# Second projection of a two-layer diffusion transformer: rows and sums split into two parts before they are stored

## The chip, the cores and the metric

The kernel runs on one core of one Trainium2 chip. The metric is the device time of one execution in microseconds (us), lower is better. Three runs of the kernel before gave 3569.83, 3571.33 and 3574.09 us, median 3571.33. The profiled execution of the same kernel took 3568.55 us.

## The reference, cut to what matters

The whole model is two layers over 256 context and 2048 latent tokens, width 1024. The change touches one product of the second layer, `h @ w_in`, where h (2304 x 1024) is the modulated layer norm of the first layer's output and the matrix gives q, k, v, o, z (1024 columns each) and 16 gates:

```python
h_lat = layer_norm(x) * (1.0 + sc_l[:, None, :]) + sh_l[:, None, :]
q, k, v, o, z, g = jnp.split(h @ w_in, ODD_SPLITS, axis=-1)
y = jax.nn.sigmoid(o) * hsum.reshape(b, t, MLSTM_W).astype(o.dtype) * jax.nn.silu(z)
```

## The kernel before, in words

Every f32 product is made of three matmuls over operands split in two parts: the high part is the value rounded to the matmul's f32 type (`ACT.Copy` into an F32R tile, on ScalarE), the low part is the value minus the high part (VectorE). `split_mm` (lines 319 to 321) adds high x high, high x low and low x high.

The second projection has two stages, each a block with a barrier at its end.

Stage one, `queries_and_sums` (tiles named `pa_`), takes 128-token tiles in pairs: eight latent pairs (0 to 7), then the context pair (8). For each tile: TensorE transposes the normalised rows (`turned`, line 1529), ScalarE and VectorE modulate half each into `ht` (lines 1401 and 1494), ScalarE makes the high part (1409), VectorE the low part (1500). Per latent pair TensorE runs four query steps of 48 matmuls and, between them, two gate products (`gates`, line 1541) into one PSUM tile, which ScalarE copies out before the next (`gate_out`, 1423). The query steps' sums are copied to `stage` (1415) and stored. The order of one pair on TensorE is: step, transposes, step, transposes, gates, step, gates, step. GpSimd forms four sums per pair from the quarters of the two tiles (1468), for a product scheme with seven products in place of eight (Strassen's, in Winograd's form), and afterwards the inverse deviations that the next pair's normalisation on VectorE waits for. It also forms three of the weight sums (`w_add`, line 1240) after pairs 3, 5 and 7, and ScalarE makes the high part of the first two of them (`w_high`, 1248) at the end of pairs 3 and 5. SyncE's queue stores to the DRAM tensor `s_hsum` three quarters of the raw rows (1335, 1337) and the four sums (1341, two buffers), whole and unsplit. Context tiles aren't split in this stage.

Stage two, `seven_products` (tiles named `pb_`), runs 34 units (four column groups over the pairs), each of seven products of 12 matmuls: 238 groups. For each group ScalarE's queue loads one 128 x 512 quarter (1659), ScalarE makes its high part (1665), VectorE its low part (1765), TensorE multiplies. Each quarter is so split anew in each column group. VectorE, ScalarE and GpSimd combine the seven results (1689 to 1797, 1743, 1747) and gate them. In the last unit of a column group ScalarE and VectorE also split the next group's weights (1248, 1253). The first unit's weights 3 to 6 are split at the stage's start; GpSimd makes the low parts of 4 and 5 (1253).

Semaphores alone set the order between engines; each engine runs its instructions in the order written. `sum_stored`, `row_stored`, `lo_done` and `mm_done` are the ones that the change touches.

## Time and profile before

| | |
|---|---|
| median of three runs | 3571.33 us |
| profiled execution, its time / its span | 3568.55 / 3566.8 us |
| TensorE matmul busy | 3367.9 us, 94% |
| VectorE, ScalarE, GpSimd busy | 66%, 38%, 50% |
| stage one (`pa_`), in the trace | about 2063 to 2289 us |
| stage two (`pb_`), in the trace | 2289 to 2981 us |

Times in the rows are microseconds from the start of the span. In a timeline a row is one or more merged instructions: start, length, engine, line, operation, tiles written and read, and in brackets the idle time of the engine just before it and what ended it. PEld is TensorE's weight load, SPq and ACTq are the DMA-issuing queues of SyncE and ScalarE. A matmul's listed length is longer than the distance between two starts, since they overlap.

### The profile page before, as it was taken

How to read it: one execution, taken by the hardware profiler on the slowest of the kernel's cores; microseconds unless marked ns; L12 is line 12 of the kernel's file. 1: busy time of each engine (PE TensorE's matmuls, PEld its weight loads, DVE VectorE, ACT ScalarE, POOL GpSimd, SP SyncE). 2: the span in 40 equal slices, each digit the busy share in tenths (PEclk: the TensorE clock that was granted, in tenths of full speed). 3: DMA queues.
4: the chain of work that ended last, by engine and by line, in shares of the span. 5: the costliest groups of instructions: out<-in, count | busy, mean ns of one | idle time of the engine just before them, and what ended most of it. 6: DMA issues, size and time to landing. Idle time of an engine off the chain costs nothing. (4 is left out here: it accounts for less than half of the span.)

```text
span 3566.8 us, 49291 instructions
## 1 busy us (share of the span) xinstructions
PE 3367.9 (94%) x16144; PEld 2481.1 (70%) x16144; DVE 2367.9 (66%) x3521; ACT 1359.8 (38%) x2274; POOL 1772.2 (50%) x1205
## 2 busy tenths in 40 slices
PE   7999998799999999999979979899999998999898
PEld 5788885555555555555568779777878786887686
DVE  4666543778877777777757754356575644779665
ACT  3433335444444444444420033334443422665300
POOL 1033312577777777777724333422575512445354
PEclk8999998799999999999989989999999999999999
DMA  5335545511111111111255555555545446768663
GB/s 206 114 110 140 139 145 171 168 33 33 37 32 35 36 34 35 36 34 35 62 172 177 175 170 181 193 191 163 172 138 170 152 148 200 218 209 274 233 229 130
DMA packets 358838, 475.43 MB, mean 133 GB/s; under 512 B 57932, under 2 KB 212444, under 8 KB 358512
## 3 DMA queue, kind: packets, MB, share of 16 engines
q1 hardware_dynamic: 300736, 359.32, 32.3%
q10 hardware_dynamic: 51600, 94.16, 8.9%
q0 software_dynamic: 6304, 19.42, 1.4%
q8 instruction: 111, 1.82, 0.2%
q14 instruction: 87, 0.71, 0.1%
HBM read 337.32 MB, written 135.36 MB: 133 GB/s over the span
## 5 line engine op out<-in xcount | busy, mean ns | idle before, releaser
L2419 DVE TENSOR_REDUCE al_mx<-al_sx 128x1 f32<-128x512 f32 (+1 forms) x960 | 559.1, 631 | 202.0 <-PE al_sx L2522 192.2
L2339 ACT ACTIVATE al_e<-al_st 128x1024 f32<-128x1024 f32 x432 | 443.3, 1027 | 535.6 <-PE al_st L2537 535.2
L2388 POOL TENSOR_TENSOR al_acc_p<-al_acc_p,al_e 128x1024 f32<-128x1024 f32 x188 | 455.7, 2424 | 19.8 <-POOL al_acc_p L2388 0.9
L319 PE MATMUL pb_acc<-p_whi,pb_r_hi 128*128 128x512 f32 x952 | 376.9, 396 | 31.7 <-DVE pb_r_lo L1765 22.4
L2546 PE MATMUL al_acc<-al_e,vres 128*64 128x512 f32 x1728 | 402.5, 601 | 0.0
L321 PE MATMUL pb_acc<-p_whi,pb_r_lo 128*128 128x512 f32 x952 | 373.7, 393 | 0.0
L320 PE MATMUL pb_acc<-p_wlo,pb_r_hi 128*128 128x512 f32 x952 | 373.6, 392 | 0.0
L2536 PE MATMUL al_st<-al_qa,kres 128*128 128x512 f32 x864 | 346.5, 401 | 3.8 <-issue 3.2
L2537 PE MATMUL al_st<-al_qb,kres 128*128 128x512 f32 x864 | 340.9, 395 | 0.0
L1765 DVE TENSOR_TENSOR pb_r_lo<-pb_stg,pb_r_hi 128x512 fp32r<-128x512 f32 x238 | 218.4, 919 | 168.5 <-ACT pb_r_hi L1665 164.5
L2522 PE MATMUL al_sx<-kres,al_qx 128*128 128x512 f32 (+1 forms) x960 | 310.7, 396 | 9.8 <-DVE al_mx L2419 7.6
L2522 PEld LDWEIGHTS al_sx<-kres,al_qx 128*128 128x128 f32 x960 | 170.7, 189 | 171.4 <-issue 114.9
L2382 POOL TENSOR_TENSOR al_acc_p<-al_e 128x1024 f32<-128x1024 f32 x48 | 160.8, 3351 | 223.9 <-ACT al_e L2339 223.9
L2546 PEld LDWEIGHTS al_acc<-al_e,vres 128*64 128x64 f32 x1728 | 111.2, 136 | 211.5 <-issue 195.6
L1665 ACT ACTIVATE pb_r_hi<-pb_stg 128x512 fp32r<-128x512 f32 x238 | 149.4, 628 | 268.3 <-PE pb_acc L321 252.0
L319 PEld LDWEIGHTS pb_acc<-p_whi,pb_r_hi 128*128 128x128 f32 x952 | 180.1, 189 | 77.2 <-DVE pb_r_lo L1765 29.1
L319 PE MATMUL mo_acc<-ow_whi,mo_y_hi 128*128 128x512 f32 x544 | 215.5, 396 | 4.9 <-DVE mo_y_lo L3088 4.9
L321 PE MATMUL mo_acc<-ow_whi,mo_y_lo 128*128 128x512 f32 x544 | 214.0, 393 | 0.0
L320 PE MATMUL mo_acc<-ow_wlo,mo_y_hi 128*128 128x512 f32 x544 | 213.9, 393 | 0.0
L2536 PEld LDWEIGHTS al_st<-al_qa,kres 128*128 128x128 f32 x864 | 162.8, 188 | 70.8 <-issue 29.1
L973 DVE TENSOR_TENSOR pj_h_lo<-pj_hall,pj_h_hi 128x1024 fp32r<-128x1024 f32 x90 | 116.4, 1310 | 138.2 <-ACT pj_h_hi L841 138.2
L321 PEld LDWEIGHTS pb_acc<-p_whi,pb_r_lo 128*128 128x128 f32 x952 | 180.1, 189 | 39.6
(344 smaller groups left out, 7411.6 us busy)
## 6 DMA issues: line engine op xcount, KB each, us to landing
pb_stg<-s_hsum ACTq DMA_DIRECT2D x238, 256.0 KB, 2.8
s_proj<-pb_out SPq DMA_DIRECT2D x72, 256.0 KB, 3.3
p_wst<-in_w1s ACTq DMA_DIRECT2D x18, 1024.0 KB, 5.5
ml_k<-s_proj SPq DMA_DIRECT2D x36, 512.0 KB, 4.4
ml_v<-s_proj SPq DMA_DIRECT2D x36, 512.0 KB, 8.9
hm_w<-in_ada_w SPq DMA_DIRECT2D x16, 1024.0 KB, 7.8
ml_qt<-s_qt SPq DMA_DIRECT2D x32, 512.0 KB, 6.4
mo_in<-s_h SPq DMA_DIRECT2D x32, 512.0 KB, 4.6
```

The source lines that it names most:

```text
L319: nc.tensor.matmul(out, s_hi, m_hi, start=start, stop=False)
L320: nc.tensor.matmul(out, s_hi, m_lo, start=False, stop=False)
L321: return nc.tensor.matmul(out, s_lo, m_hi, start=False, stop=stop)
L1765: V.tensor_tensor(r_lo[:, g % RING], stg[:, g % NSTG], r_hi[:, g % RING].bitcast(F32), ALU.subtract).then_inc(lo_done, 1)
L2339: nc.scalar.activation(e[:, pair(p, j), :, :], st[(NP * p + j) % 2][:, :, 0:W], ACT.Exp).then_inc(e_done, 1)
L2382: nc.gpsimd.tensor_tensor(acc_p[:], e[:, pair(p, 2)], e[:, pair(p, 5)], ALU.add).then_inc(add_p, 1)
L2388: nc.gpsimd.tensor_tensor(acc_p[:], acc_p[:], e[:, pair(p, j)], ALU.add).then_inc(add_p, 1)
L2419: V.tensor_reduce(mx[:, x:x + 1], slots[x % NSX][:, 0:spans[x % NS][1]], AX.X, ALU.max).then_inc(sx_max, 1)
L2522: mm(slots[x % NSX][:, 0:width], qx[:, p, i * P:(i + 1) * P], kres[:, g, lo:lo + width], start=True, stop=True).then_inc(sx_mm, 1)
L2536: mm(dst[:, t, 0:W], kres[:, g, keys], qa[:, p, :], start=True, stop=False)
L2537: y = mm(dst[:, t, 0:W], kres[:, NKV + g, keys], qb[:, p, :], start=False, stop=True)
L2546: y = mm(acc[t * HD:(t + 1) * HD, 0:W], vres[:, 2 * j + t, g, :], e[:, pair(p, j), t, :], start=(j == 0), stop=(j == NP - 1))
```

## The change

It moves the splits of rows and sums from stage two into stage one. `s_hsum` doubles in size: each quarter now has a high and a low plane (`(NT // 2, 7, P, 2, CH)`).

Stage one now splits the context tiles too. The stores of rows read `h_hi` and `h_lo` (four DMAs a pair instead of two, twice the bytes), so `ht` is freed without waiting for a store, and `h_hi`/`h_lo` wait for it instead. GpSimd's four sums have a buffer each (`sums`, four places), ScalarE writes the high part to `sum_hi` (two places), VectorE subtracts in place. These splits of a pair's sums stand one pair later in each engine's order (`early_splits`), but those of pair 7 in pair 7 (`late_splits`) and those of pair 8 at the end. A sum's split in a `sum_hi` place waits until the place's last content is stored. The loads of the next rows (`load_x`) are issued ahead of the sums' stores. `stage` has two places instead of three.

Stage two loads both parts of a quarter in one DMA of 512 KB into a ring of six (instead of four raw and four split), with no split; TensorE waits for the DMA. Weights 4 and 5 of the first unit get their low parts on VectorE, and the order of the weights' splits there is 3, 4, 5, 6.

ScalarE, stage one, from the end of pair 3 into pair 4. `pa_stage` is the copy of a query step, `p_whi` the high part of the weight sum, `pa_ht` a modulated tile, `pa_h_hi` its high part, `pa_gst` the copy of a gate product.

```order
L1415 ACTIVATE pa_stage<-pa_acc 128x512
L1248 ACTIVATE p_whi<-p_wst 128x2048
L1415 ACTIVATE pa_stage<-pa_acc 128x512
L1401 ACTIVATE pa_ht<-pa_tp,keep_mod 128x128 x4
L1409 ACTIVATE pa_h_hi<-pa_ht 128x1024
L1415 ACTIVATE pa_stage<-pa_acc 128x512
L1401 ACTIVATE pa_ht<-pa_tp,keep_mod 128x128 x4
L1409 ACTIVATE pa_h_hi<-pa_ht 128x1024
L1423 ACTIVATE pa_gst<-pa_gacc,pa_gbias 128x128
```

The same place after the change:

```order
L1420 ACTIVATE pa_stage<-pa_acc 128x512
L1248 ACTIVATE p_whi<-p_wst 128x2048
L1420 ACTIVATE pa_stage<-pa_acc 128x512
L1436 ACTIVATE pa_sum_hi<-pa_sums 128x512 x2
L1407 ACTIVATE pa_ht<-pa_tp,keep_mod 128x128 x4
L1414 ACTIVATE pa_h_hi<-pa_ht 128x1024
L1420 ACTIVATE pa_stage<-pa_acc 128x512
L1436 ACTIVATE pa_sum_hi<-pa_sums 128x512 x2
L1407 ACTIVATE pa_ht<-pa_tp,keep_mod 128x128 x4
L1414 ACTIVATE pa_h_hi<-pa_ht 128x1024
L1428 ACTIVATE pa_gst<-pa_gacc,pa_gbias 128x128
```

Two pairs of splits of the pair before now stand ahead of the two modulations, and so ahead of the gate copy that TensorE's second gate product waits for.

SyncE's queue, stage one, its last DMAs, from the store of the third query step of pair 7 on. Before:

```order
L1352 DMA s_qt<-pa_stage 128x2x256
L1346 DMA s_graw<-pa_gst 128x128
L1341 DMA s_hsum<-pa_sums 128x512 x2
L1352 DMA s_qt<-pa_stage 128x2x256
L1346 DMA s_graw<-pa_gst 128x128 x2
```

After:

```order
L1363 DMA s_qt<-pa_stage 128x2x256
L1357 DMA s_graw<-pa_gst 128x128
L1352 DMA s_hsum<-pa_sum_hi 128x512
L1352 DMA s_hsum<-pa_sums 128x512
L1352 DMA s_hsum<-pa_sum_hi 128x512
L1352 DMA s_hsum<-pa_sums 128x512
L1363 DMA s_qt<-pa_stage 128x2x256
L1352 DMA s_hsum<-pa_sum_hi 128x512
L1352 DMA s_hsum<-pa_sums 128x512
L1352 DMA s_hsum<-pa_sum_hi 128x512
L1352 DMA s_hsum<-pa_sums 128x512
L1357 DMA s_graw<-pa_gst 128x128
```

Behind the last query store (`s_qt`) stood two gate stores. Now there stand four stores of the context pair's sums 0 and 1, a gate store, and behind these rows four more of its sums 2 and 3 and the last gate store.

VectorE at the start of stage two. Before:

```order
L1765 TENSOR_TENSOR pb_r_lo<-pb_stg,pb_r_hi 128x512 x2
L1253 TENSOR_TENSOR p_wlo<-p_wst,p_whi 128x2048
L1765 TENSOR_TENSOR pb_r_lo<-pb_stg,pb_r_hi 128x512 x3
L1780 TENSOR_TENSOR pb_u<-pb_acc,pb_s 128x512
```

After:

```order
L1253 TENSOR_TENSOR p_wlo<-p_wst,p_whi 128x2048 x2
L1233 TENSOR_TENSOR p_wst<-p_wst 128x2048
L1253 TENSOR_TENSOR p_wlo<-p_wst,p_whi 128x2048 x2
L1790 TENSOR_TENSOR pb_u<-pb_acc,pb_s 128x512
```

All four low parts of weights and the last weight sum (1233) now stand ahead of the first result.

```diff
-        self.ops = q + [(0, i) for i in (0, 2, 1, 3, 4, 6, 5)] + [(p, i) for p in range(1, 4) for i in range(7)]
+        self.ops = q + [(0, i) for i in (0, 2, 1, 3, 4, 5, 6)] + [(p, i) for p in range(1, 4) for i in range(7)]
...
-    tag, NX, RING, NH, NACC, NST = "pa_", 2, 4, 4, 3, 3
+    tag, NX, RING, NH, NACC, NST = "pa_", 2, 4, 4, 3, 2
...
-    sums = m.sb(tag + "sums", [P, 2, 4, P])
+    sums, sum_hi = m.sb(tag + "sums", [P, 4, 4, P], F32R), m.sb(tag + "sum_hi", [P, 2, 4, P], F32R)
...
+    sum_done, sum_stored, row_stored = m.sem(tag + "sum"), m.sem(tag + "sum_stored", 4), m.sem(tag + "row_stored")
+    sum_hi_done, sum_lo_done = m.sem(tag + "sum_hi"), m.sem(tag + "sum_lo")
+    early_splits = lambda pair, b: [(pair - 1, 2 * b), (pair - 1, 2 * b + 1)] if 0 < pair < LAT else [(LAT, 2 * b), (LAT, 2 * b + 1)] if pair == LAT else []
+    late_splits = lambda pair, b: [(pair, 2 * b), (pair, 2 * b + 1)] if pair == LAT - 1 else []
...
-            eng.wait_ge(row_stored, 32 * pair + 32)
-            if pair < LAT:
-                eng.wait_ge(hi_done, i - NH + 1)
-                eng.wait_ge(lo_done, i - NH + 1)
+            eng.wait_ge(hi_done, i - NH + 1)
+            eng.wait_ge(lo_done, i - NH + 1)
+
+    def split_free(eng, i):
+        if i >= RING:
+            eng.wait_ge(mm_done, 4 * ((i - RING) // 2 + 1))
+            eng.wait_ge(row_stored, 64 * ((i - RING) // 2 + 1))
...
             def rows(pair):
-                modulated(sp, 2 * pair)
                 view = s["hsum"][pair]
-                sp.dma_start(view[0:2].rearrange("o p f -> p o f"), ht[:, 2 * pair % NH].rearrange("p (o k) n -> p o (k n)", o=2)).then_inc(row_stored, 16)
-                modulated(sp, 2 * pair + 1)
-                sp.dma_start(view[2], ht[:, (2 * pair + 1) % NH, 4:KD].rearrange("p k n -> p (k n)")).then_inc(row_stored, 16)
-
-            def sum_out(pair, n):
-                sp.wait_ge(sum_done, 4 * pair + n + 1)
-                sp.dma_start(s["hsum"][pair, 3 + n], sums[:, n % 2].rearrange("p k n -> p (k n)")).then_inc(sum_stored[n % 2], 16)
+                for i in (2 * pair, 2 * pair + 1):
+                    for part, (done, t) in enumerate(((hi_done, h_hi), (lo_done, h_lo))):
+                        sp.wait_ge(done, i + 1)
+                        if i % 2 == 0:
+                            sp.dma_start(view[0:2, :, part].rearrange("o p f -> p o f"), t[:, i % RING].rearrange("p (o k) n -> p o (k n)", o=2).bitcast(F32)).then_inc(row_stored, 16)
+                        else:
+                            sp.dma_start(view[2, :, part], t[:, i % RING, 4:KD].rearrange("p k n -> p (k n)").bitcast(F32)).then_inc(row_stored, 16)
+
+            def sum_out(pair, q):
+                sp.wait_ge(sum_lo_done, 4 * pair + q + 1)
+                view = s["hsum"][pair, 3 + q]
+                for part, t in enumerate((sum_hi[:, q % 2], sums[:, q])):
+                    sp.dma_start(view[:, part], t.rearrange("p k n -> p (k n)").bitcast(F32)).then_inc(sum_stored[q], 16)
...
             for pair in range(LAT):
                 last = pair == LAT - 1
                 rows(pair)
-                sum_out(pair, 0)
-                sum_out(pair, 1)
-                query_out(4 * pair)
-                if not last:
-                    load_x(2 * pair + 4)
-                sum_out(pair, 2)
-                query_out(4 * pair + 1)
-                if not last:
-                    load_x(2 * pair + 5)
-                sum_out(pair, 3)
-                gate_out(2 * pair)
-                if last:
-                    rows(PAIRS - 1)
-                    sum_out(PAIRS - 1, 0)
-                    sum_out(PAIRS - 1, 1)
-                query_out(4 * pair + 2)
-                gate_out(2 * pair + 1)
-                if last:
-                    sum_out(PAIRS - 1, 2)
-                    sum_out(PAIRS - 1, 3)
-                query_out(4 * pair + 3)
+                for b in range(2):
+                    query_out(4 * pair + b)
+                    if not last:
+                        load_x(2 * pair + 4 + b)
+                    for of in early_splits(pair, b):
+                        sum_out(*of)
+                for b in range(2):
+                    gate_out(2 * pair + b)
+                    for of in late_splits(pair, b):
+                        sum_out(*of)
+                    if last and b == 0:
+                        rows(PAIRS - 1)
+                    query_out(4 * pair + 2 + b)
                 if pair in (1, 2, 4, 6):
                     w.w_load(sp, (0, {1: 0, 2: 2, 4: 1, 6: 3}[pair]))
-            gate_out(2 * LAT)
-            gate_out(2 * LAT + 1)
+            for b in range(2):
+                for of in early_splits(LAT, b):
+                    sum_out(*of)
+                gate_out(2 * LAT + b)
...
+            def sum_high(pair, q):
+                act.wait_ge(sum_done, 4 * pair + q + 1)
+                if q >= 2:
+                    act.wait_ge(sum_stored[q - 2], 32 * pair + 32)
+                elif pair:
+                    act.wait_ge(sum_stored[q + 2], 32 * pair)
+                nc.scalar.activation(sum_hi[:, q % 2], sums[:, q].bitcast(F32), ACT.Copy).then_inc(sum_hi_done, 1)
...
                     i = 2 * pair + 2 + b
                     if q:
                         query_out(4 * pair + b)
+                    for of in early_splits(pair, b):
+                        sum_high(*of)
                     if i < NT:
                         modulate(i)
-                        if i < 2 * LAT:
-                            high(i)
+                        high(i)
                 for b in range(2):
                     gate_out(2 * pair + b)
+                    for of in late_splits(pair, b):
+                        sum_high(*of)
                     if q:
                         query_out(4 * pair + 2 + b)
...
-                terms = ((a21, a22, ALU.add), (sums[:, 0], a11, ALU.subtract), (a11, a21, ALU.subtract), (a12, sums[:, 1], ALU.subtract))
-                for n, (p, q, op) in enumerate(terms):
-                    if pair or n >= 2:
-                        pool.wait_ge(sum_stored[n % 2], 16 * (2 * pair + n // 2))
-                    if n:
-                        pool.wait_ge(sum_done, 4 * pair + n)
-                    G.tensor_tensor(sums[:, n % 2], p, q, op).then_inc(sum_done, 1)
+                place = [sums[:, n].bitcast(F32) for n in range(4)]
+                terms = ((a21, a22, ALU.add), (place[0], a11, ALU.subtract), (a11, a21, ALU.subtract), (a12, place[1], ALU.subtract))
+                for q, (x, y, op) in enumerate(terms):
+                    if pair:
+                        pool.wait_ge(sum_stored[q], 32 * pair)
+                    if q:
+                        pool.wait_ge(sum_done, 4 * pair + q)
+                    G.tensor_tensor(place[q], x, y, op).then_inc(sum_done, 1)
...
+            def sum_low(pair, q):
+                dve.wait_ge(sum_hi_done, 4 * pair + q + 1)
+                if q < 2:
+                    dve.wait_ge(sum_done, 4 * pair + (2, 4)[q])
+                place = sums[:, q]
+                V.tensor_tensor(place, place.bitcast(F32), sum_hi[:, q % 2].bitcast(F32), ALU.subtract).then_inc(sum_lo_done, 1)
...
+    tag, RING = "pb_", 6
...
             def load(g):
                 u, i = divmod(g, 7)
-                if g >= NSTG:
-                    act.wait_ge(lo_done, g - NSTG + 1)
-                act.dma_start(stg[:, g % NSTG].rearrange("p k n -> p (k n)"), s["hsum"][UNITS[u][1], w.ROWS[i]]).then_inc(ld[g % NSTG], 16)
-
-            def high(g):
-                act.wait_ge(ld[g % NSTG], 16 * (g // NSTG) + 16)
                 if g >= RING:
                     act.wait_ge(mm_done, g - RING + 1)
-                nc.scalar.activation(r_hi[:, g % RING], stg[:, g % NSTG], ACT.Copy).then_inc(hi_done, 1)
+                act.dma_start(rows[:, g % RING].rearrange("p w k n -> p w (k n)").bitcast(F32), s["hsum"][UNITS[u][1], w.ROWS[i]]).then_inc(ld[g % RING], 16)
...
                 nc.scalar.activation(sg[:, at % 2], out[:, kind], ACT.Sigmoid).then_inc(sg_done[kind], 1)

-            for g in range(NSTG):
+            for g in range(3):
                 load(g)
-            for g in range(2):
-                high(g)
             w.w_high(act, (0, 3))
-            for g in range(2, RING):
-                high(g)
-            for g in range(NSTG, NSTG + RING - 1):
+            for g in range(3, RING):
                 load(g)
+            w.w_high(act, (0, 4))
...
-                if j + NSTG + RING - 1 < N:
-                    load(j + NSTG + RING - 1)
-                if j in (0, 2, 3):
-                    w.w_high(act, (0, {0: 4, 2: 6, 3: 5}[j]))
+                if j + RING < N:
+                    load(j + RING)
...
-            for g in range(2):
-                low(g)
             w.w_low(V, (0, 3))
-            for g in range(2, RING):
-                low(g)
+            w.w_low(V, (0, 4))
+            w.w_add(V, 0, 5)
+            w.w_low(V, (0, 5))
+            w.w_low(V, (0, 6))
...
-                pe.wait_ge(lo_done, j + 1)
+                pe.wait_ge(ld[j % RING], 16 * (j // RING) + 16)
...
-        "hsum": dram("s_hsum", (NT // 2, 7, P, CH)),
+        "hsum": dram("s_hsum", (NT // 2, 7, P, 2, CH)),
```

## Rows read from the trace of the kernel before

**Rows 1.** Windows, stage two: length, busy and count per engine, PEclk, DMA share, GB/s.

```profile
2450.00:2500.00 50.00, 46.07 (x200) 37.09 (x199) 37.78 (x35) 25.26 (x29) 7.36 (x5) 1.00 0.52 164
2500.00:2550.00 50.00, 50.00 (x221) 41.20 (x220) 25.48 (x35) 20.68 (x35) 23.04 (x25) 1.00 0.55 171
2600.00:2650.00 50.00, 46.36 (x200) 36.85 (x198) 36.64 (x33) 26.30 (x34) 32.05 (x26) 1.00 0.46 142
2650.00:2700.00 50.00, 47.69 (x206) 38.62 (x207) 30.42 (x34) 21.97 (x37) 32.99 (x30) 1.00 0.48 134
2800.00:2850.00 50.00, 45.89 (x191) 35.91 (x190) 35.05 (x37) 21.14 (x30) 19.85 (x13) 0.97 0.58 184
```

**Rows 2.** Waits of TensorE in stage two: us in total, times, longest.

```profile
PE pb_acc L319 <- DVE pb_r_lo L1765: 22.4, 15, 7.9
```

**Rows 3.** Timeline of TensorE, end of stage one and first seven groups.

```profile
2285.87 0.64 PE L1541 MATMUL pa_gacc<-pa_ht,pa_wg 128*32 128x128 f32 x16 [0.49 <-ACT pa_gst L1423]
...
2294.38 0.79 PE L319 MATMUL pb_acc<-p_whi,pb_r_hi 128*128 128x512 f32 x1 [7.87 <-DVE pb_r_lo L1765]
...
2299.66 0.63 PE L319 MATMUL pb_acc<-p_whi,pb_r_hi 128*128 128x512 f32 x1
...
2320.81 0.77 PE L319 MATMUL pb_acc<-p_whi,pb_r_hi 128*128 128x512 f32 x1 [8.65 <-POOL p_wlo L1253]
...
2325.36 0.39 PE L319 MATMUL pb_acc<-p_whi,pb_r_hi 128*128 128x512 f32 x1
```

**Rows 4.** Timeline of ScalarE and its queue, start of stage two.

```profile
2289.11 2.05 ACTq L1659 DMA_DIRECT2D pb_stg<-s_hsum  x4
...
2292.97 0.63 ACT L1665 ACTIVATE pb_r_hi<-pb_stg 128x512 fp32r<-128x512 f32 x1 [6.02 <-DMA pb_stg<-s_hsum]
...
2295.69 0.63 ACT L1665 ACTIVATE pb_r_hi<-pb_stg 128x512 fp32r<-128x512 f32 x1 [2.09 <-DMA pb_stg<-s_hsum]
```

**Rows 5.** Tile pb_stg: count, ns min/median/max, first and last start, forms.

```profile
L1665 ACT ACTIVATE pb_r_hi<-pb_stg x238: 608/632/635, 2293.0 to 2970.8; 128x512 fp32r<-128x512 f32 x119
L1765 DVE TENSOR_TENSOR pb_r_lo<-pb_stg,pb_r_hi x238: 672/692/4677, 2293.6 to 2971.4; 128x512 fp32r<-128x512 f32 x119
```

**Rows 6.** Timeline of stage one, ScalarE, GpSimd and VectorE, pair 4.

```profile
2179.99 0.60 ACT L1415 ACTIVATE pa_stage<-pa_acc 128x512 f32<-128x512 f32 x1 [5.54 <-PE pa_acc L321]
...
2182.39 1.92 ACT L1248 ACTIVATE p_whi<-p_wst 128x2048 fp32r<-128x2048 f32 x1 [1.80 <-POOL p_wst L1240]
...
2185.71 0.60 ACT L1415 ACTIVATE pa_stage<-pa_acc 128x512 f32<-128x512 f32 x1 [1.40 <-PE pa_acc L321]
...
2193.25 1.51 ACT L1401 ACTIVATE pa_ht<-pa_tp,keep_mod 128x128 f32<-128x128 f32 x4 [0.36 <-PE pa_tp L1529]
...
2199.69 0.60 ACT L1415 ACTIVATE pa_stage<-pa_acc 128x512 f32<-128x512 f32 x1 [3.53 <-PE pa_acc L321]
...
2206.20 0.60 ACT L1415 ACTIVATE pa_stage<-pa_acc 128x512 f32<-128x512 f32 x1 [5.54 <-PE pa_acc L321]
...
2176.86 5.50 POOL L1240 TENSOR_TENSOR p_wst<-p_wst 128x512 f32<-128x512 f32 x4
...
2176.94 1.77 DVE L1288 TENSOR_SCALAR p_x<-p_x,p_mv,p_rstd 128x1024 f32<-128x1024 f32 x1 [0.94 <-POOL p_rstd L1274]
...
2195.93 1.23 DVE L1500 TENSOR_TENSOR pa_h_lo<-pa_ht,pa_h_hi 128x1024 fp32r<-128x1024 f32 x1 [1.30 <-ACT pa_h_hi L1409]
```

**Rows 7.** Timeline of TensorE, the first query step, started after an idle stretch.

```profile
2072.27 0.58 PE L319 MATMUL pa_acc<-pa_h_hi,p_whi 128*128 128x256 f32 x1 [6.95 <-DVE pa_h_lo L1500]
...
2075.38 0.28 PE L321 MATMUL pa_acc<-pa_h_hi,p_wlo 128*128 128x256 f32 x1
```

**Rows 8.** DMA issues: KB each, landing; one sum store, then all tile pa_sums.

```profile
s_hsum<-pa_sums SPq DMA_DIRECT2D x1, 256.0 KB, 2.1
...
DMA to landing us min/median/max: 2.0/3.5/8.8
```

**Rows 9.** Timeline of SyncE's queue, the last stores of stage one.

```profile
2285.88 1.41 SPq L1346 DMA_DIRECT2D s_graw<-pa_gst  x2
```

40 lines of the change are left out of this document (15 added, 25 removed).

## The prediction

> **What bounds the kernel now.** I read the table of the page first: TensorE works 94% of the span, so a change pays only where TensorE stands or runs slowly. The windows of stage two show where that is. An undisturbed window of 50 us holds 221 matmuls, 0.226 us each, so a group of 12 takes 2.72 us [rows 1]. Four windows, around the three changes of column group, hold 200, 200, 206 and 191. The list of waits names the low parts of the rows on VectorE [rows 2], and the timeline of the stage's start shows the rest: the first group starts at 2294.38, TensorE then stands 8.65 us for GpSimd's low part of a weight, and the seventh group starts only at 2325.36 [rows 3]. In stage one TensorE hardly stands at all. A pair takes 26.2 us, from the copy at 2179.99 to the one at 2206.20 [rows 6], and nearly all of it is its own work. So stage two has something to give, and stage one can only lose.
>
> **Stage two, changes of column group.** Removed are 238 high parts of 0.63 us on ScalarE and 238 low parts of 0.69 us on VectorE [rows 5], busy time beside TensorE that is worth nothing by itself. At a change VectorE has, for seven groups (19 us), seven low parts of weights, one weight sum, five results and seven low parts of rows, and TensorE waits for the last kind only a few groups after. Now TensorE needs a weight's low part seven groups after its old one is used, and has six result banks (16 us) of patience. VectorE's remaining work is still over 19 us, but lags by less than that. Short of 221 are 21, 21, 15 and 30 matmuls: 87 x 0.226 = 19.7 us [rows 1]. I take all of it; the bounds are 12 and 21 (a small fifth stretch isn't counted).
>
> **Stage two, its start.** Before, stage start to seventh group: 2325.36 - 2289.11 = 36.3 us [rows 3, 4]. After: the first DMA carries 512 KB. The old loads of 256 KB could be split 3.9 and 6.6 us after the start, beside two loads of weights [rows 4]; the new one is both together, so between 3.9 and 6.6, and I take 5.8, nearer to the second. The 1.4 us of splitting behind it (2292.97 to 2294.38) goes. First group at 5.9. It runs at the low of the two clock levels for 5.3 us as before (2294.38 to 2299.66) [rows 3], the second partly (3.2, estimate), then four at 2.72: seventh group at 25.3 us. The weights' low parts would be ready in time: VectorE makes four of 2.3 us and a sum of 3.4 one behind another and ends some 22 to 23 us after the start. Gain 11.0 us, bounds 8 and 12. DMA: 96 GB/s more on windows of 134 to 184 [rows 1] stays below the 300 to 400 that the start of the stage reaches, and loads are issued five groups (13.6 us) ahead, so I price it at nothing; without that cover see the last rival. Stage two: -30.7 us.
>
> **Stage one, an ordinary pair.** Let t be 0 where a pair's first query step starts. ScalarE copies it at 5.7. Now two high parts of sums come first (0.6 each), so modulation ends at 9.0, its high part at 10.1, VectorE's low part (1.23) at 11.4 and the low part of sum 0 at 12.1. Both its stores are out by 12.5. A lone store landed in 2.1 us, the median of all 36 is 3.5 [rows 8]. I take 2.7 us from low part to landing, second issue included. Sum 2's high part reuses sum 0's place and so waits until 14.7, those of 2 and 3 end at 16.1, the modulation at 17.6, the high part at 18.7, the gate copy at 19.1. TensorE wants it at 19.7 (2199.69 - 2179.99) [rows 6]: no wait, 0.6 us to spare. I put 0.5 us for all such pairs; bounds 0 and 8.
>
> **Stage one, pairs 4 and 6.** ScalarE ends pairs 3 and 5 with the high part of a weight sum that GpSimd makes behind its row sums and inverse deviations. Before, it could start at t = 2.4 of the next pair (2182.39) and ended at 4.3, unnoticed [rows 6]. Now GpSimd's third row sum must wait for the stored sum 2 of the pair before: VectorE's low part of it at 20.7, landed 23.4; two row sums 26.2; two inverse deviations, each 0.94, with VectorE's normalisation between them, 30.4; weight sum 5.5 [rows 6], 35.9, which is 9.7 in the next pair. ScalarE's high part ends at 11.6. Queued behind it stand the copy (12.2), two high parts (13.4), modulation and high part (16.7, since VectorE too held a weight's low part), a copy (17.3); VectorE's low part and sum's low part 18.6; landed 21.3, both high parts 22.6, modulation 24.1, high part 25.2, gate copy 25.6. TensorE has waited since 19.7: 5.9 us. After pair 5 VectorE has no such weight, 5.2 us. Sum 11.1; bounds 5 (a landing of 2.0 and ScalarE's weight wait half as long) and 18 (landings of 3.5). Each such stop also costs clock. After 6.95 us of idling 14 matmuls took 3.11 us [rows 7] where a query step of 48 in 5.72 us [rows 6] gives 1.67: 1.4 us, twice, 2.8; nothing if the clock holds.
>
> **Stage one, its end.** Pair 7 starts at 2179.99 + 3 x 26.2 = 2258.6. The stage ended with a gate store issued by 2287.3 [rows 9] and stage two began at 2289.11, t = 30.5 [rows 4]. Now the sums of pairs 7 and 8 are split one after another in two places, each waiting for a landing. Sum 2 of pair 6 landed 23.4; pair 7: high parts of 0 and 1 at 24.0 and 24.7, landed 27.4 and 29.6 (VectorE's low part of sum 1 waits for GpSimd's fourth, 26.2); high parts of 2 and 3 28.0 and 30.2. Sum 2's stores stand behind four of rows (1.5 MB), so I give it 4.7 us from issue at 30.3, between the median and the longest [rows 8]: 35. Pair 8: GpSimd, after the third weight sum (31.7), waits for that landing with its third sum, and ends at 37.8. High parts of 0 and 1 at 35.6 and 36.9, landed 39.0 and 41.2; of 2 and 3 at 39.6 and 41.8; low part 42.5, landed 45.2, stage end 45.6. That is 15.1 us more. VectorE's operations run longer beside GpSimd's (1.77 us for a normalisation that stands beside a weight sum [rows 6]); I add 2: 17 us, bounds 13 and 24. The Trainium skill, "DMA: Bandwidth & Descriptors", section on the anatomy of one DMA, fits a DMA from GpSimd's queue as about 2.0 us plus its bytes over 436 GB/s, 2.6 us for 256 KB. The trace's lone store is half a microsecond shorter. By the page's figure each landing in the chains above would be 0.5 us later and the total about 6 us higher.
>
> **The sum.** 0.5 + 11.1 + 2.8 + 17 = 31.4 lost, 30.7 won: +0.7 us on the profiled execution's 3568.55. That one lies 2.8 us below the median of the runs (3571.33), to which I add the difference: **3572.0 us**. With the bounds nearest at hand, 3566 to 3579. The measurement tells about 0.2% (7 us) from no change.
>
> **Rivals.**
> - *The stops in stage one don't reach TensorE* (faster). For it: before, ScalarE waits for TensorE most of the time in stage one. Against: its order is fixed, and the spare time is 0.6 us. Without 11.1 and 2.8: 3558.
> - *Stores land slowly* (slower). This is one mechanism: the two-place buffer of high parts turns each landing into a wait. It decides from 2.7 us from low part to landing on; at 3.5 plus the second issue, 1.3 more, it costs in pairs 4 and 6 3 landings each (7.8), in five ordinary pairs 0.7 each (3.5), and six landings at the end (7.8): +19, 3591. For it: the median of 3.5, and 1.8 MB more to store per pair. Against: these stores stand alone in the queue, as the one of 2.1 did.
> - *Row loads come late* (slower): 512 KB in 2.72 us, and weights of 1 MB in the same queue. A few microseconds at each of three changes and at the start, about 8: 3580. Against it the 13.6 us of lead.
>
> **Chances.** Forecast 0.42, slow stores 0.27, stops not seen 0.24, late loads 0.07. The range takes in the first three cases up to just below the slow one's middle: 3558 to 3590. Faster by over 0.2% has the third case and the low end of the forecast, 0.27; slower has the slow stores but for their low end, some of the late loads and the high end of the forecast, 0.32; the same 0.41.
>
> **What would show it.** Windows of about 221 matmuls at the column changes and no wait for a low part of rows there. A seventh group some 25 us after stage two's start. In stage one two waits of TensorE's gate products for the gate copy, of 5 to 6 us, in pairs 4 and 6, with ScalarE before them waiting for GpSimd's weight sum; ScalarE waiting for `s_hsum` stores in every pair; 40 us or more between the start of pair 7 and the next stage. The prediction is wrong if TensorE passes pairs 4 and 6 unhindered, if the end of stage one takes as long as before, or if TensorE waits for row loads in stage two.

## The result

The changed kernel is slower: ratio to the kernel before 1.0077, 95% interval 1.0055 to 1.0099 (median 3599.71 us of five runs, 3588.62 to 3606.72; before 3570.34). Run once more beside other variants it gave 1.0055 (1.0035 to 1.0076), median 3595.18 us. The profiled execution took 3606.72 us, span 3604.6, the slowest of the five. Of the 38 us between it and the profiled execution of before, 4.9 lie ahead of the stretches below and 5.6 behind them, in parts of the program that the change does not touch.

For each kernel three stretches can be read from the trace. *Pairs*: from ScalarE's fourth copy of pair 0 to the start of the last query product. *End*: from there to stage two's first load. *Stage two*: from there to the start of its last product. The last two columns are the sum of the three against the kernel before (879.5 us), and the measured ratio. The rows below the second are the variants of the section on the experiments.

| kernel | pairs | end | stage two | sum | ratio (95%) |
|---|---|---|---|---|---|
| before | 183.2 | 4.6 | 691.7 | | |
| changed | 209.8 | 24.9 | 672.2 | +27.4 | 1.0077 (1.0055 to 1.0099) |
| changed, again | 209.4 | 25.0 | 669.5 | +24.4 | 1.0055 (1.0035 to 1.0076) |
| room | 194.2 | 22.4 | 669.6 | +6.7 | 1.0012 (0.9997 to 1.0027) |
| gap | 198.2 | 25.6 | 666.7 | +11.0 | 1.0055 (1.0036 to 1.0075) |
| lag | 208.9 | 24.9 | 661.1 | +15.4 | 1.0047 (1.0030 to 1.0064) |
| vlow | 205.7 | 25.0 | 666.5 | +17.7 | 1.0049 (1.0031 to 1.0066) |
| x_last | 208.8 | 25.1 | 673.9 | +28.3 | 1.0057 (1.0036 to 1.0078) |
| lag_before | 183.2 | 4.6 | 681.2 | -10.5 | 0.9954 (0.9937 to 0.9970) |
| start_before | 183.2 | 4.5 | 685.1 | -6.7 | 0.9984 (0.9970 to 0.9997) |
| lag_start_before | 183.2 | 4.6 | 674.8 | -16.9 | 0.9951 (0.9932 to 0.9970) |
| all | 183.2 | 24.9 | 661.2 | -10.2 | 0.9960 (0.9943 to 0.9976) |
| all_late | 183.2 | 23.4 | 661.2 | -11.7 | 0.9948 (0.9933 to 0.9963) |
| all_vadd | 183.2 | 20.7 | 661.0 | -14.6 | 0.9937 (0.9918 to 0.9956) |

So stage two gave 19.5 us, and stage one cost 26.6 in its pairs and 20.3 at its end.

The sums come from one trace each and the ratios from six or more executions (the changed kernel's first from five); they differ by up to 9 us. Six traces have the changed kernel's stage two unaltered (`changed` twice, `room`, `gap`, `vlow`, `x_last`): it took 666.5 to 673.9 us there, mean 669.7. The four with `lag` took 661.0 to 661.2. The part on `lag` shows where the difference comes from.

**The profile after, stage one.** An ordinary pair, pair 1: ScalarE, VectorE's low parts of sums 0 and 1, then SyncE's queue.

```profile
2111.95 0.60 ACT L1420 ACTIVATE pa_stage<-pa_acc 128x512 f32<-128x512 f32 x1 [5.12 <-PE pa_acc L321]
2112.45 1.14 ACT L1436 ACTIVATE pa_sum_hi<-pa_sums 128x512 fp32r<-128x512 f32 x2
...
2118.53 0.60 ACT L1420 ACTIVATE pa_stage<-pa_acc 128x512 f32<-128x512 f32 x1 [2.41 <-PE pa_acc L321]
2122.97 0.63 ACT L1436 ACTIVATE pa_sum_hi<-pa_sums 128x512 fp32r<-128x512 f32 x1 [3.84 <-DMA s_hsum<-pa_sums]
2124.40 0.63 ACT L1436 ACTIVATE pa_sum_hi<-pa_sums 128x512 fp32r<-128x512 f32 x1 [0.80 <-POOL pa_sums L1485]
...
2127.47 0.35 ACT L1428 ACTIVATE pa_gst<-pa_gacc,pa_gbias 128x128 f32<-128x128 f32 x1
```

```profile
2117.30 1.29 DVE L1524 TENSOR_TENSOR pa_sums<-pa_sums,pa_sum_hi 128x512 fp32r<-128x512 f32 x2
```

```profile
2118.02 0.32 SPq L1352 DMA_DIRECT2D s_hsum<-pa_sum_hi  x1
2118.38 0.43 SPq L1352 DMA_DIRECT2D s_hsum<-pa_sums  x1
2118.86 2.25 SPq L1352 DMA_DIRECT2D s_hsum<-pa_sum_hi  x1
```

Count t from the fourth copy of the pair before (2106.23); the first copy then stands at 5.7, as in the prediction. The first two high parts start at 6.2. The low part of sum 0 ends at 2117.97 and is stored at once, and the third high part, which needs its place, starts at 2122.97: 5.0 us of landing, where I took 2.7. The place is read by the store of the high part alone, which landed 2.5 us after its issue (2118.02), at t = 14.3. But both stores of a sum count on one semaphore, and ScalarE waits for both; the low part's landed 4.5 us after its issue (2118.38). The gate copy follows at t = 21.2; TensorE needed it at 19.7. By the same rows of the other pairs the landing is 3.1 us in pair 2 (where the second pair of stores lands later still), 4.1 in pair 5, 2.9 in pair 7, and the gate copy stands at 20.7, 20.2 and 19.1. Pairs 1, 2, 5 and 7 last 29.7, 27.7, 27.3 and 26.2 us (pair 7 by TensorE's start of its last query product); 26.2 is the pair of before [rows 6].

Pair 3 lasts 31.5. Here are VectorE's normalisation and GpSimd's low part of a weight at its start, then ScalarE's high part of the weight sum in pair 4 and TensorE's waits for the gate copy (us in total, times, longest) from 2075 to 2330, which leaves out the last one, 18.2 us at the stage's end.

```profile
2168.17 5.10 DVE L1288 TENSOR_SCALAR p_x<-p_x,p_mv,p_rstd 128x1024 f32<-128x1024 f32 x1 [0.94 <-POOL p_rstd L1274]
```

```profile
2168.09 4.63 POOL L1253 TENSOR_TENSOR p_wlo<-p_wst,p_whi 128x2048 fp32r<-128x2048 f32 x1
```

```profile
2203.76 1.92 ACT L1248 ACTIVATE p_whi<-p_wst 128x2048 fp32r<-128x2048 f32 x1 [8.00 <-POOL p_wst L1240]
```

```profile
PE pa_gacc L1569 <- ACT pa_gst L1428: 20.8, 8, 6.2
```

The normalisation takes 0.81 us alone and 1.77 beside a weight sum. Here it lasts as long as GpSimd's operation beside it, and pair 3's first low part of a sum comes 2.1 us late. In pair 4 ScalarE ends the weight's high part at 2205.68, t = 10.5 (I had 11.6), and the pair lasts 33.3; pair 6 lasts 34.3. Before, the wait for the gate copy in [rows 3] is 0.49, and all of them in stage one are 1.6.

The end of stage one, GpSimd: the weight sum stands in front of pair 8's sums, and the third of them (2328.03) waits for a store of pair 7.

```profile
2316.86 5.82 POOL L1240 TENSOR_TENSOR p_wst<-p_wst 128x512 f32<-128x512 f32 x4
2322.65 1.70 POOL L1485 TENSOR_TENSOR pa_sums<-pa_ht 128x512 f32<-128x512 f32 x1
2324.50 1.26 POOL L1485 TENSOR_TENSOR pa_sums<-pa_sums,pa_ht 128x512 f32<-128x512 f32 x1
2328.03 1.26 POOL L1485 TENSOR_TENSOR pa_sums<-pa_ht 128x512 f32<-128x512 f32 x1 [2.27 <-DMA s_hsum<-pa_sums]
```

**Stage two after.** The windows that answer to [rows 1]: three with a change of column group and one without.

```profile
2500.00:2550.00 50.00, 47.53 (x202) 38.71 (x201) 27.92 (x21) 17.47 (x14) 11.07 (x7) 0.97 0.79 262
2550.00:2600.00 50.00, 50.00 (x221) 41.10 (x220) 8.30 (x12) 10.01 (x17) 22.59 (x27) 1.00 0.80 265
2650.00:2700.00 50.00, 47.79 (x203) 38.88 (x202) 27.61 (x19) 20.86 (x21) 36.48 (x27) 0.97 0.69 229
2800.00:2850.00 50.00, 47.61 (x210) 38.89 (x209) 26.12 (x19) 20.87 (x21) 35.35 (x27) 1.00 0.72 234
```

TensorE's waits in stage two, answer to [rows 2], and its timeline: first group, sixth, seventh [rows 3], and the stop at the first change.

```profile
PE pb_acc L319 <- DMA pb_rows<-s_hsum: 9.1, 1, 9.1
PE pb_acc L319 <- DVE pb_out L1802: 7.1, 3, 2.5
PE pb_acc L319 <- DVE p_wlo L1253: 1.4, 1, 1.4
```

```profile
2345.73 0.80 PE L319 MATMUL pb_acc<-p_whi,pb_rows 128*128 128x512 f32 x1 [9.12 <-DMA pb_rows<-s_hsum]
...
2363.38 0.47 PE L319 MATMUL pb_acc<-p_whi,pb_rows 128*128 128x512 f32 x1 [1.36 <-DVE p_wlo L1253]
...
2366.69 0.47 PE L319 MATMUL pb_acc<-p_whi,pb_rows 128*128 128x512 f32 x1 [0.30 <-issue]
...
2531.49 0.68 PE L319 MATMUL pb_acc<-p_whi,pb_rows 128*128 128x512 f32 x1 [2.47 <-DVE pb_out L1802]
```

The stage starts with the load of 2340.86: first group after 4.9 us, seventh after 25.8 (before 36.3). The waits for low parts of rows are gone. In their place stand three waits for a result of VectorE, and behind the first of them TensorE runs for 3 us at the lower of its two clock levels (2531.97 to 2534.96, 0.63 us a matmul where it takes 0.39). What VectorE and ScalarE do ahead of the first:

```profile
2518.12 0.39 ACTq L1220 DMA_DIRECT2D p_wst<-in_w1s  x1
...
2525.70 1.92 ACT L1248 ACTIVATE p_whi<-p_wst 128x2048 fp32r<-128x2048 f32 x1 [7.93 <-DMA p_wst<-in_w1s]
```

```profile
2527.66 2.29 DVE L1253 TENSOR_TENSOR p_wlo<-p_wst,p_whi 128x2048 fp32r<-128x2048 f32 x1 [4.64 <-ACT p_whi L1248]
2529.86 0.68 DVE L1799 TENSOR_TENSOR pb_out<-pb_acc,pb_u 128x512 f32<-128x512 f32 x1
2530.65 0.69 DVE L1802 TENSOR_TENSOR pb_out<-pb_acc,pb_out 128x512 f32<-128x512 f32 x1
```

Weight 4 of the next column group is loaded only now and lands 7.6 us later. ScalarE's high part, VectorE's low part and, behind them in the order, results whose products are long done wait for it, until TensorE has no free bank.

### The profile page after: what moved, and what is told of

The parts are those of the page before. It is cut to its first block and busy times, and to the rows that moved or that the text cites. A ratio compares the mean times of both kernels' runs of the same rounds, so it can differ in the third digit from the quotient of the medians.

```text
span 3604.6 us, 48847 instructions
## 1 busy us (share of the span) xinstructions
PE 3385.7 (94%) x16144; PEld 2497.2 (69%) x16144; DVE 2181.4 (61%) x3323; ACT 1243.2 (34%) x2074; POOL 1739.4 (48%) x1203
## 3 DMA queue, kind: packets, MB, share of 16 engines
q1 hardware_dynamic: 309664, 375.84, 33.3%
## 5 line engine op out<-in xcount | busy, mean ns | idle before, releaser
L319 PE MATMUL pb_acc<-p_whi,pb_rows 128*128 128x512 f32 x952 | 375.3, 394 | 17.9 <-DMA pb_rows<-s_hsum 9.1
L321 PE MATMUL pb_acc<-p_whi,pb_rows 128*128 128x512 f32 x952 | 373.4, 392 | 0.0
L320 PE MATMUL pb_acc<-p_wlo,pb_rows 128*128 128x512 f32 x952 | 373.2, 392 | 0.0
L319 PEld LDWEIGHTS pb_acc<-p_whi,pb_rows 128*128 128x128 f32 x952 | 180.0, 189 | 58.5 <-issue 10.7
L321 PEld LDWEIGHTS pb_acc<-p_whi,pb_rows 128*128 128x128 f32 x952 | 180.0, 189 | 40.0
L320 PEld LDWEIGHTS pb_acc<-p_wlo,pb_rows 128*128 128x128 f32 x952 | 180.1, 189 | 38.3
L2541 PEld LDWEIGHTS al_st<-al_qb,kres 128*128 128x128 f32 x864 | 163.0, 189 | 30.2
```

The lines of the kernel that those rows point to most:

```text
L319: nc.tensor.matmul(out, s_hi, m_hi, start=start, stop=False)
L320: nc.tensor.matmul(out, s_hi, m_lo, start=False, stop=False)
L321: return nc.tensor.matmul(out, s_lo, m_hi, start=False, stop=stop)
L2541: y = mm(dst[:, t, 0:W], kres[:, NKV + g, keys], qb[:, p, :], start=False, stop=True)
```

## The experiments

**changed, again.**

> The changed kernel once more, unaltered, so that the variants are compared with runs of the same day. If the difference of 27 us is the kernel's: a ratio of 1.0055 to 1.0099 again. The variants lag, gap and vlow lay 4 to 9 us lower than their traces explain from 3599.7; if that median was high by chance, it comes out near 3592 now.

1.0055, and +24.4 us in its trace. The two intervals overlap from 1.0055 to 1.0076: the difference is the kernel's, and the first median may have been somewhat high.

Against this second ratio, of the variants of the changed kernel that have one alteration, `room` alone is told apart by its time. `gap`, `lag`, `vlow` and `x_last` (1.0047 to 1.0057) are not; what they show, they show in the lengths of pairs and stages in their traces.

### Stage one

**room.** High parts of pairs 0 to 3 go to `whi[1]`, a place for a weight that is still empty then, two of pair 7 and two of pair 8 to `x`, the place of the rows. The stores, the low parts and the waits follow (not shown):

```diff
+    def high_place(pair, q):
+        if pair < 4:
+            return w.whi[1][:, q]
+        if pair == LAT - 1 and q >= 2:
+            return x[:, 0, (q - 2) * CH:(q - 1) * CH].bitcast(F32R)
+        if pair == LAT and q < 2:
+            return x[:, 1, q * CH:(q + 1) * CH].bitcast(F32R)
+        return flat(sum_hi[:, q % 2])
```

> High parts of the sums get more places: those of pairs 0 to 3 go to the weight slot that is still empty then, those of pair 7 (two) and pair 8 (two) to the two places of x that are free by then; pairs 4, 5, 6 keep the two places. Theory (each high part of sums 2 and 3 waits for a store to land, 2.9 to 5.0 us, and the gate copy behind it comes late): pairs 1 to 4, which now last 3.5, 1.5, 5.3 and 7.1 us longer than before, lose nearly all of that, pairs 5 and 6 (1.0 and 8.1) keep theirs, the end of stage one gets 5 to 7 us shorter. About 23 us off the changed kernel's 3599.7: 3577. Rival (the stops come from the doubled bytes of the stores and from VectorE running beside GpSimd): less than 5 us, 3595 to 3600, the stops in pairs 1 to 4 stay.

Pair 1 of this kernel, ScalarE:

```profile
2109.69 0.60 ACT L1431 ACTIVATE pa_stage<-pa_acc 128x512 f32<-128x512 f32 x1 [2.41 <-PE pa_acc L321]
2110.18 1.14 ACT L1460 ACTIVATE p_whi<-pa_sums 128x512 fp32r<-128x512 f32 x2
...
2113.77 0.35 ACT L1439 ACTIVATE pa_gst<-pa_gacc,pa_gbias 128x128 f32<-128x128 f32 x1
```

The gate copy stands at t = 16.4, 4.9 us earlier. Pairs 1 to 4 last 26.2, 26.2, 26.2 and 26.8 us; pairs 5 and 6, which keep the two places, 27.7 and 35.2. All bytes are stored as before, so the waiting for a place is the cause in pairs 1 to 4 and the bytes are not. Pair 3's slow normalisation is gone too: it starts 0.5 us ahead of GpSimd's low part of the weight (2151.78 against 2152.29) and takes 0.81 us. And the weight sum is as late as before in pair 4 (first high part at t = 10.7), so a late weight sum alone costs 0.6 us there. The end got only 2.5 us shorter, where I expected 5 to 7.

**gap.**

```diff
                     G.tensor_tensor(place[q], x, y, op).then_inc(sum_done, 1)
+                    if q == 1 and pair in (3, 5, 7):
+                        w.w_add(G, 0, {3: 2, 5: 1, 7: 3}[pair])
...
-                elif pair in (3, 5, 7):
-                    w.w_add(G, 0, {3: 2, 5: 1, 7: 3}[pair])
```

> The changed kernel with GpSimd's weight sums moved from behind its row sums into the wait between the second and the third row sum of the same pair. Theory (ScalarE stands 8.0 and 9.3 us for the late weight sum, and everything in pairs 4 and 6 stands behind it): pair 4's stop goes from 7.1 to about 3.5, what pair 1 has, and pair 6's from 8.1 to about 2.5; the end does not change, because GpSimd's third sum of pair 8 waits for a landing there. About 9 us off: 3590. Rival (the moved sum slows VectorE's low parts in the middle of the pair and the landing waits fill the time): under 3 us.

Pair 4 went from 33.3 to 26.3 us, more than expected, pair 6 from 34.3 to 31.6, less: there a 5.10 us normalisation now stands beside GpSimd's low part of weight 1. In pair 4 the late weight sum and the wait for a place make the stop together: `room` takes the second away and `gap` the first, and each alone brings the pair to 26.8 and 26.3. In pair 6 the edit takes 2.7 us of 8.1 away. The end did not get shorter (25.6). Pair 1, which this edit leaves as it was, took 27.9 us in place of 29.7; in `vlow` and `lag` it took 27.9 and 28.0.

**vlow.** The two low parts leave GpSimd (the lines that go are not shown). VectorE has, between its modulation and its low part of the second token tile, the lines below; they also move weight 2's low part from the end of pair 3 into pair 4.

```diff
+                        if i % 2 and pair in (3, 4, 6):
+                            w.w_low(V, (0, {3: 0, 4: 2, 6: 1}[pair]))
```

> The changed kernel with the low parts of the weights 0 and 1 taken from GpSimd (behind its row sums in pairs 2 and 5) and done by VectorE, with that of weight 2, while it waits for the second high part in pairs 3, 4 and 6. Theory (the normalisation that runs beside GpSimd's low part takes 5.10 us and 0.81 otherwise, and sets back the first low part of pair 3 by 2.1 us; then the landing waits come on top): pair 3 goes from 31.5 us to about 28.5, pair 6 by 1 us or less because ScalarE stands there for the weight sum. About 4 us off the changed kernel: 3596 at 3599.7, the landing waits of 3 to 5 us stay. Rival (the two engines do not disturb each other, the long normalisation is a wait for something else): pair 3 keeps its 31.5 us.

Pair 3 went from 31.5 to 28.0 us; pair 4 took 34.6 in place of 33.3, pair 6 stayed (34.4). The contention was worth 3.5 us. The next pair gave 1.3 back; weight 2's low part stands in it now, and whether that is the reason is not shown.

**x_last.** `load_x` behind the `sum_out` calls in SyncE's order.

> The changed kernel with each load of x (512 KB) issued behind the four stores of sums that follow it, not in front of them. It tells what makes these stores land late in pairs 1, 2, 3, 5 (second high parts at t = 16.7, 14.9, 18.4, 15.8 in place of the 14.6 of pair 7, which loads no x). Theory (the load in front of them holds the stores up in the one queue): second high parts of pairs 1, 2 and 5 at 14.6 to 14.9, and these three pairs last 26.2 to 26.7 us where they took 29.7, 27.7 and 27.3; about 6 us off the kernel's time. Rival (the 1.5 MB of rows, or nothing in that queue): the pairs keep their lengths within 0.5 us.

Pair 1 27.4 (29.7), pair 2 27.8 (27.7), pair 3 32.3 (31.5), pair 5 26.4 (27.3), pair 6 35.5 (34.3), no gain in total. In pair 5, which took 27.3 or 27.4 us in five traces, the load in front held the stores up by 0.9 us. Pair 1 took 29.7 us in the two traces of the changed kernel, but 27.9 to 28.0 in `gap`, `vlow` and `lag`, which do not touch it; so about 0.5 us of its gain is the most that can be put down to the load. What makes the stores land after 3 to 5 us stays open.

### Stage two

**lag.** The high and low parts of weights 4, 5 and 6 of the next column group come one group later, on ScalarE and on VectorE.

```diff
                     if last_unit(u):
-                        w.w_high(act, (p, i))
+                        if i != 4:
+                            w.w_high(act, (p, i if i < 4 else i - 1))
...
+                if u and last_unit(u - 1) and i == 0:
+                    w.w_high(act, (UNITS[u][0], 6))
...
-                    w.w_low(V, op)
+                    if i != 4:
+                        w.w_low(V, (op[0], i if i < 4 else i - 1))
...
+                if u and last_unit(u - 1) and i == 1:
+                    w.w_low(V, (UNITS[u][0], 6))
```

> The changed kernel with the high and low parts of the weights 4, 5 and 6 of the next column group taken one group later, behind the results of that group. Theory (at each change VectorE waits for the low part of the weight whose load has just been issued, 7.5 us to landing, and its results stand behind that until TensorE has no free bank): the three waits of 2.47, 2.21 and 2.39 us for the result of line 1802 and the slow clock behind them go, and the windows at the changes hold 221 matmuls where they hold 202, 203 and 210. 48 x 0.226 = 10.8 us at most; I expect 9: 3591. Rival (the landing of the weights itself is the bound, whatever stands in front): TensorE waits for a low part of a weight in the new column group instead, gain under 3 us.

TensorE's waits in its stage two are

```profile
PE pb_acc L319 <- DMA pb_rows<-s_hsum: 9.1, 1, 9.1
PE pb_acc L319 <- DVE p_wlo L1253: 1.7, 1, 1.7
```

The result's waits are gone, the windows at all three changes hold 220 to 222 matmuls, stage two is 11.1 us shorter than in the first run of the changed kernel, 8.4 than in the second, and 5 to 13 shorter than in the six traces without the edit. The blocking was the whole rest at the changes.

The six traces without the edit show the landing at work by itself. They hold 18 changes of column group, in which weight 4 landed 5.0 to 8.1 us after its issue. In the four where it took 5.0 to 5.1, TensorE did not stop. In the others the stop grows with the landing, microsecond for microsecond (`changed` has 7.6, 7.3 and 7.5; the rest are from all six):

| landing | 5.1 | 5.7 | 6.7 | 7.0 | 7.3 | 7.6 | 8.1 |
|---|---|---|---|---|---|---|---|
| TensorE's stop | 0 | 0.6 | 1.6 | 1.9 | 2.2 | 2.5 | 2.9 |

This is why stage two varies from 666.5 to 673.9 us in kernels that have the same code there, and why it does not with `lag`.

**lag_before.** The same edit in the kernel before.

> The same reordering of weights 4, 5, 6 in the kernel before the change, whose rows are still split in stage two. Theory (there VectorE is short of time, not blocked: it idles only about 2.4 us in a change of column group): under 5 us gained, 3566 to 3571, and the waits for the low parts of rows stay. Rival (the blocking by the weight's landing was the cost in the kernel before too, and the split of the rows was not): 10 us or more, 3560.

```profile
PE pb_acc L319 <- DVE pb_r_lo L1768: 14.2, 12, 7.8
```

I was wrong here: 10.5 us in stage two, ratio 0.9954. The wait under the name of the rows' low parts falls from 22.4 [rows 2] to 14.2 us, of which 7.8 and 7.9 are the stage's start. So 8.1 of the 14.5 us at the changes hung on the order of the weights' splits. The kernel before, first change, ScalarE and VectorE; the last row is the low part that releases TensorE after 2.48 us:

```profile
2483.82 1.92 ACT L1248 ACTIVATE p_whi<-p_wst 128x2048 fp32r<-128x2048 f32 x1 [2.65 <-DMA p_wst<-in_w1s]
...
2485.77 2.29 DVE L1253 TENSOR_TENSOR p_wlo<-p_wst,p_whi 128x2048 fp32r<-128x2048 f32 x1 [1.25 <-ACT p_whi L1248]
...
2489.37 0.68 DVE L1765 TENSOR_TENSOR pb_r_lo<-pb_stg,pb_r_hi 128x512 fp32r<-128x512 f32 x1
```

VectorE stands 1.25, 1.20 and 1.29 us for the landing at the three changes, 3.7 in total. The rest of the 8.1 is work: the weight's low part (2.29 us) in front of the rows' low part, which the edit also moves away. No run separates the two. The other 6.4 were the splitting of rows: in `lag`, where the split is stored and the order is the same, TensorE waits for nothing there.

**start_before** and **lag_start_before.** The kernel before with the start of stage two in the new order, rows still split there, without and with `lag`:

```diff
-                if j in (0, 2, 3):
-                    w.w_high(act, (0, {0: 4, 2: 6, 3: 5}[j]))
+                if j in (0, 1, 2):
+                    w.w_high(act, (0, 4 + j))
...
-                if j in (0, 3):
-                    w.w_low(G, (0, 5 if j else 4))
...
-                if j == 2:
-                    w.w_low(V, (0, 6))
+                if j in (0, 1, 2):
+                    w.w_low(V, (0, 4 + j))
```

> The kernel before with only the start of stage two reordered (low parts of weights 4 and 5 on VectorE, order 4, 5, 6). Theory (the wait of 8.65 us for GpSimd's low part was the order's, not the split's): the group that started 31.7 us after the stage starts after 25.5, stage two 6 us shorter, 3564 where the kernel before has 3570; the three changes of column group stay as they are. Rival (VectorE's later low parts of rows give it back): within 2 us of the kernel before, with waits for the low parts of rows in the first three groups of seven.

> The kernel before, rows split in stage two as before, with weights 4, 5, 6 of a column group one group later, and at the start of stage two the low parts of weights 4 and 5 on VectorE, in the order 4, 5, 6, in place of GpSimd. Theory (the gain at the start comes from taking GpSimd's 4.6 us low parts away, beside which VectorE's operations take 4.6 and 4.4 us in place of 0.69, and not from the stored split): the seventh group starts about 27 us after the stage, not 36.3; 8 to 10 us on top of the 16.5: 3543. Rival (VectorE, with seven rows' and four weights' low parts and a sum, is the bound there): 3550 or more, TensorE waits for low parts of rows.

```profile
2307.04 0.47 PE L319 MATMUL pb_acc<-p_whi,pb_r_hi 128*128 128x512 f32 x1 [4.46 <-DVE p_wlo L1253]
```

In `start_before` the stage starts at 2281.64; the group that stood for GpSimd's low part (31.7 us after the start, [rows 3, 4]) starts after 25.4, stage two is 6.6 us shorter, the time 0.16% less. With `lag` the trace gains 16.9 us, the ratio is no better than `lag_before`'s: the two intervals overlap nearly whole. The 8 to 10 us that I expected at the start were 6.4 (681.2 - 674.8). So of the 10.5 us that the start gained in the changed kernel, about 6 need no stored split. In all of stage two the stored split is worth 674.8 - 661.1 = 13.7 us beside both reorderings.

### Together

**all** (a place for each high part, `gap`, `vlow`, `lag`; weight 1's high and low part one pair later than in `vlow`), **all_late**, **all_vadd**, each on top of the one before. The last moves pair 7's weight sum from GpSimd to VectorE (`w.w_add(V, 0, 3)`), the middle one puts `rows(PAIRS - 1)` behind `late_splits(pair, 1)` on SyncE.

> The changed kernel with everything at once: a place of its own for each high part of a sum (the empty weight slot for pairs 0 to 5, the two places of x for two sums each of pairs 6, 7, 8), weight sums in the wait between the second and third row sum, weights' low parts on VectorE, weights 4, 5, 6 of a column group one group later. Theory: all seven pairs last 26.2 us, the stretch from the last product of stage one to stage two's first load is 15 to 17 us (24.7 in the changed kernel, 4.3 in the kernel before), stage two lasts 661 us. 11 to 13 lost and 30 won against the kernel before: 3550, near the reordered kernel before (3552.6). Rival (the doubled bytes cost by themselves: stores and loads slow each other): pairs above 27 us or stage two above 668, 3565 or more.

> As `all`, and in pair 7 SyncE issues the stores of pair 7's sums 2 and 3 before those of pair 8's rows. Theory (GpSimd's third sum of pair 8 waits for the store of pair 7's third, whose issue stands behind four stores of 1.5 MB): the end of stage one gets 2 to 3 us shorter than in `all`. Rival (the four stores of rows are then what lands last, the end stays or gets 1 us longer).

> `all_late` with the weight sum of pair 7 on VectorE in place of GpSimd, in front of pair 7's low parts. Theory (the end of stage one is GpSimd's chain: 5.5 us of weight sum stand in front of pair 7's third row sum, and pair 8's wait for the stores of pair 7's): the stretch from stage one's last product to stage two's first load falls from 23.1 to about 14 us, the time from 3551 to 3542. Rival (the stretch is set by the bytes to be stored, 1.5 MB of rows and 4 MB of sums at 360 to 400 GB/s in about 15 us, behind each other in one queue): it stays above 20 us, 3549 or more.

All seven pairs last 26.2 us and stage two 661: as expected, and the rival of the bytes is out for both. The end is not: 24.9, 23.4 and 20.7 us where I expected 15 to 17, 2 to 3 less, and 14. In `all_vadd` GpSimd's first row sum of pair 7, beside VectorE's low parts and weight sum, lasts

```profile
2281.22 8.06 POOL L1504 TENSOR_TENSOR pa_sums<-pa_ht 128x512 f32<-128x512 f32 x1 [12.36 <-DVE pa_ht L1526]
```

and from 2300 to 2310 the DMA engines move 373 to 382 GB/s: so both the chain and the bytes may hold the end there; no run separates them. `all_vadd` has the lowest ratio, 0.9937; by its interval it cannot be told from `all_late`, `lag_start_before` and `lag_before`. All of these beat the kernel before and the changed one. But the best of them with the stored split is no better than the kernel before with its two stages' orders mended (`lag_start_before`): by the traces, the 13.7 us that the split saves in stage two are outweighed by the 16.1 that the end of stage one costs in `all_vadd` (20.7 against 4.6). The gain on the kernel before is that of the order; that the stored split adds anything is not shown.

## Why the prediction was wrong

Forecast 3572.0 us, range 3558 to 3590; measured 3599.7 (3595.2 the second time, outside the range too). By its own terms, in us (prediction, trace):

| term | predicted | in the trace |
|---|---|---|
| changes of column group | -19.7 | -8.8 |
| start of stage two | -11.0 | -10.5 |
| ordinary pairs (1, 2, 3, 5, 7) | +0.5 | +11.3 |
| stops in pairs 4 and 6, with the clock | +13.9 | +15.2 |
| end of stage one | +17 | +20.3 |
| sum | +0.7 | +27.5 |

- *Changes of column group: the step that failed.* "I take all of it" rested on reading the wait for `pb_r_lo` as a shortage of VectorE alone, which ends with the split of the rows. Short of 221 are now 19, 18 and 11 matmuls, 48 x 0.226 = 10.8 us, against 19.7. In the changed kernel TensorE waits for results that stand behind a weight's low part, and that waits for a landing: ScalarE stands 7.9, 7.6 and 7.8 us for weight 4 at the three changes, VectorE 4.6, 2.8 and 3.0 us behind it. `lag` takes the stops away, and the stops follow the landing. I had priced the DMA at nothing in this stage. Before, VectorE stood 1.2 to 1.3 us for it at each change and was short of time for the rest, so my reading was right in part there (`lag_before`). The claim that VectorE's work lags by less than six banks counted its work and not its waits. The term was 10.9 us too large by this trace, and its 8.8 lie below my bound of 12. Over the six traces without `lag`, whose landings differ, stage two lies 5 to 13 above that of `lag`.
- *Ordinary pairs: the other one.* 0.5 us, with a bound of 8; the spare time of 0.6 us was right to the tenth (pair 7: gate copy at 19.1, no stop). The landing was mis-sized, 2.9 to 5.0 us in place of 2.7, and in pair 3 VectorE came late, which made 3.5 of its 5.3 us (`vlow`). `room` takes the landing out and the stops go. I had counted both stores of a sum and did not ask which of them reads the place: by the landings of the high parts alone, pairs 2 and 5 would have had their third and fourth high parts by t = 15.7 and no stop, and pair 1 a shorter one (an estimate from the trace; no run has a semaphore for each store). A stop costs more than its wait. Pair 1's copy is 1.5 us late and the pair 3.5 longer: TensorE stands for 2.0 us of it, and behind the stop 18 matmuls start 0.21 us apart in place of 0.12 (2128.5 to 2132.2, granted clock 0.55), which is 1.6.
- *Slow stores.* The rival was the right mechanism, from the point that I gave (2.7 us) on, and had 0.27. Its price of 19 us was spread over pairs 4 and 6 and the end; it came mainly in the ordinary pairs (3.5 expected in five, 11.3 there). By it alone 3591.
- *Pairs 4 and 6, start, end.* As worked out: the stops in the place named, for the weight sum (`gap`), seventh group after 25.8 us (25.3 expected), 50.8 us from the start of pair 7 to stage two (47.6). The end was 3.3 us over, inside its bounds. In pair 4 the weight sum alone would not have stopped TensorE (`room`): that the two mechanisms need each other is in the chain of the prediction, which has a landing in it, but was not said.
- *Row loads come late* had 0.07 and a price of 8 us, a few at each change. No row load held TensorE up after the first group, but the weights in the same queue, which that rival named too, did: the 10.9 us at the changes are theirs. *The stops in stage one don't reach TensorE*: wrong, TensorE stops in each of pairs 1 to 6.
- *The range* ended at the rival's middle. Two independent terms could both fail upwards, and I had given that no share.

The Trainium skill, "SBUF — State Buffer", section "SBUF: two separate sides", says that VectorE and GpSimd share a pair of ports, and that the one that comes first holds it for its whole instruction, if VectorE's runs in a two-port mode or has two inputs in SBUF while GpSimd's reads SBUF. The trace agrees: a normalisation of 0.81 us, started 0.08 us behind a GpSimd operation of 4.63, took 5.10. The row sum of 1.29 us took 8.06 beside a run of VectorE operations with two inputs each, from 2281.10 to 2288.13, and so waited for more than one instruction. Which mode the normalisation runs in, no trace shows. In the prediction I had put 2 us for it at the end only; by that rule, each GpSimd operation that the later row sums push against VectorE's had to be asked for its full length, and `vlow` prices the one in pair 3 at 3.5 us.

## What to carry to other kernels

The name in a list of waits is the last instruction of a queue; before a wait is booked as that instruction's work, look at what stands in front of it on its engine and whether that works or waits. An in-order engine should not stand for a transfer just issued while results that free buffers stand behind it; how much that costs then changes from one execution to the next with the landing: taking three weights' splits one group later gained 0.5% in the kernel before, for no byte moved. A buffer of two places that turns a store's landing into a wait on the critical engine's path needs its price at the longest landing the queue shows, and its places can be borrowed from buffers that are empty at that time. A comparison of the repaired change needs the repaired kernel before beside it.
